# A wide form for two output units of each mixer, with the weights of the next unit but one prepared ahead of its eviction

## What is computed

```python
for i in range(DEPTH):                    # 4 layers: nsa, moba, conv, nsa
    x = x + mixer_i(rms_norm(x))          # ends in  o @ w_out,  1024 x 1024
    h = rms_norm(x)
    x = x + (silu(h @ w_gate) * (h @ w_up)) @ w_down
```

## Time and profile before

| | us |
|---|---|
| median of 3 runs | 2200.45 (2199.61 to 2200.75) |
| time of the profiled execution | 2200.64 |
| its span, first to last instruction | 2198.8 |
| PE busy | 2172.7 |
| DVE busy | 1783.2 |
| ACT busy | 1170.8 |

### The profile page before, as it was taken

One profiled execution on the slowest core, in us unless ns is written; L12 is line 12 of the kernel. 1 busy time (PEld: TensorE's weight loads), 2 busy tenths in 40 slices (PEclk: granted clock), 3 DMA queues, 4 the chain that ended last, 5 costly groups with the idle time before them and its releaser, 6 DMA issues.

```text
span 2198.8 us, 38037 instructions
## 1 busy us (share of the span) xinstructions
PE 2172.7 (99%) x15141; PEld 1946.7 (89%) x15141; DVE 1783.2 (81%) x3522; ACT 1170.8 (53%) x2051; POOL 0.2 (0%) x4
## 2 busy tenths in 40 slices
PE   9999999999999999999999999999999999999998
PEld 8888889898899988996988887898888889979998
DVE  8879978689887898888898777578877876478898
ACT  5776556565554655558655646453222236376533
POOL 0000000000000000000000000000000000000000
PEclk9999999999999999999999999999999999999999
DMA  8326665466665666670676531015454523435663
GB/s 272 123 84 235 222 213 193 166 210 234 196 220 176 208 237 201 220 222 22 229 236 201 178 125 58 20 61 181 157 187 167 166 80 106 135 98 166 208 236 120
DMA packets 115377, 372.04 MB, mean 169 GB/s; under 512 B 12416, under 2 KB 22272, under 8 KB 115200
## 3 DMA queue, kind: packets, MB, share of 16 engines
q1 hardware_dynamic: 106688, 359.97, 49.4%
q10 hardware_dynamic: 8512, 9.63, 1.4%
HBM read 367.46 MB, written 1.05 MB: 168 GB/s over the span
## 4 chain that ended last, share of the span: by engine, by line
PE 91%; DVE 6%; ACT 2%; issue 1%; DMA 0%; ACTq 0%; DVEq 0%; SPq 0%
PE ps L538 88%; DVE hid_f L2564 1%; PE ps L882 1%; DVE hid_f L2586 1%; PE ps L818 1%; PE ps L866 1%; DVE w_lo L2169 1%; PE ps L988 0%; ACT p_ring L1620 0%; DVE X L2301 0%; PE ps L806 0%; DVE a_both L2169 0%; DVE X L2448 0%; DVE recip L2580 0%; ACT hid_f L1687 0%
## 5 line engine op out<-in xcount | busy, mean ns | idle before, releaser
L538 PE MATMUL ps<-a_both,w_hi 128*128 128x256 f32 (+1 forms) x4816 | 1028.3, 328 | 1.4 <-DVE a_both L2169 0.7
L538 PEld LDWEIGHTS ps<-a_both,w_hi 128*128 128x128 f32 x4816 | 806.0, 190 | 78.0 <-DVE a_both L2169 3.4
L2169 DVE TENSOR_TENSOR w_lo<-w_raw,w_hi 128x1024 fp32r<-128x1024 f32 (+3 forms) x630 | 704.3, 1145 | 74.3 <-ACT w_hi L1480 58.3
L538 PE MATMUL ps<-a_both,w_lo 128*128 128x256 f32 (+1 forms) x3112 | 693.5, 292 | 0.0
L1480 ACT CAST w_hi<-w_raw 128x1024 fp32r<-128x1024 f32 (+3 forms) x428 | 403.8, 973 | 270.8 <-DMA w_raw<-weights 269.3
L538 PEld LDWEIGHTS ps<-a_both,w_lo 128*128 128x128 f32 x3112 | 506.3, 191 | 17.3
L538 PE MATMUL ps<-hid_both,w_hi 128*128 128x512 f32 (+2 forms) x2184 | 513.0, 347 | 0.7 <-DVE hid_both L2361 0.2
L538 PEld LDWEIGHTS ps<-hid_both,w_hi 128*128 128x128 f32 x2184 | 377.5, 189 | 54.4 <-issue 5.4
L538 PE MATMUL ps<-hid_both,w_lo 128*128 128x256 f32 (+2 forms) x1444 | 329.9, 304 | 0.0
L538 PEld LDWEIGHTS ps<-hid_both,w_lo 128*128 128x128 f32 x1444 | 229.8, 191 | 14.2
L1488 ACT CAST w_hi<-w_raw 128x1024 fp32r<-128x1024 f32 (+1 forms) x198 | 202.4, 1022 | 0.3 <-DMA w_raw<-weights 0.3
(11 more groups left out here) (261 smaller groups left out, 1938.9 us busy)
## 6 DMA issues: line engine op xcount, KB each, us to landing
w_raw<-weights SPq DMA_DIRECT2D x496, 512.0 KB, 4.5
pe_sb<-weights SPq DMA_DIRECT2D x96, 512.0 KB, 5.4
w_raw<-weights SPq DMA_DIRECT2D x64, 384.0 KB, 3.3
w_raw<-weights SPq DMA_DIRECT2D x64, 320.0 KB, 3.7
pe_sb<-na_bias ACTq DMA_DIRECT2D x32, 128.0 KB, 2.2
X<-x_t SPq DMA_DIRECT2D x2, 512.0 KB, 6.9
X<-c_rows ACTq DMA_DIRECT2D x2, 512.0 KB, 7.6
qk<-qk ACTq DMA_DIRECT2D x4, 256.0 KB, 6.2
```

The source lines that it names most:

```text
L538: return nc.tensor.matmul(out, stationary, moving, start=start, stop=stop)
L2169: return v.tensor_tensor(out, a, b.bitcast(F32), ALU.subtract)
```

## The change

Units o1 and o2 of all four mixers take the wide form. Unit o2 goes to ring A, o1 and o3 stay in D. PE issues all 16 high products of the unit, then the 16 low ones (`wide_unit`). On ACT and DVE, `mixer_ends` for these two units calls `ahead(u)` first; then ACT copies the low halves of both tiles in one instruction of 512 columns into `low_slot`, and DVE adds that copy to both tiles of `X` (512 columns, SBUF only), waits for itself, and adds the high halves from PSUM (512 columns). The tile work behind it is the same. Units o0 and o3 stay as they were, with `ahead(u)` behind.

```diff
+MIXER_WIDE = (1, 2)
...
+        def bank_pair(made):
+            lower = min(bank for bank, _, _ in made)
+            return slice(lower, lower + 2)
...
+            def wide_unit(ring, xs):
+                u, made = start_unit(2 * ring)
+                for _, p, _ in made:
+                    start_product(ring, p)
+                lower = bank_pair(made).start
+                for bank, _, _ in made:
+                    wide_highs(ps[:, bank, :], u % SLOTS, (bank - lower) * KD, xs, True, False)
+                for bank, _, (ready, _) in made:
+                    wide_lows(ps[:, bank, :], u % SLOTS, (bank - lower) * KD, xs, True).then_inc(ready, 1)
...
+                    if both and i in MIXER_WIDE:
+                        wide_unit("DA"[i - 1], both)
+                        continue
...
             def mixer_ends(gain, first="D"):            # ACT
+                before = None
                 for i in range(4):
-                    ring = first if i == 0 else "D"
+                    ring = first if i == 0 else "DAD"[i - 1]
                     u, made = next_unit(2 * ring)
                     if i == 3:
                         ready_sqrt()
+                    if i in MIXER_WIDE:
+                        ahead(u)
+                        for _, _, (s_, count) in made:
+                            wait(act, s_, count)
+                        if before:
+                            act.wait_ge(taken[before[0]], before[1] + 1)
+                        before = ring, made[1][1]
+                        nc.scalar.copy(low_slot, ps[:, bank_pair(made), S:2 * S]).then_inc(low_copied, 1)
                     for m in range(2):
                         residual_tile(made[m], 2 * i + m, gain, ring)
-                    ahead(u)
+                    if i not in MIXER_WIDE:
+                        ahead(u)
...
             def mixer_ends(gain, first="D"):            # DVE
+                    if i in MIXER_WIDE:
+                        ahead(u)
+                        for m in made:
+                            ready(m)
+                        n["low_part"] += 1
+                        dve.wait_ge(low_copied, n["low_part"])
+                        x = X[:, 2 * i:2 * i + 2, LAT]
+                        step(v.tensor_tensor(x, x, low_slot, ALU.add))
+                        sync()
+                        v.tensor_tensor(x, ps[:, bank_pair(made), 0:S], x, ALU.add).then_inc(taken[ring], 2)
+                    for m in range(2) if i not in MIXER_WIDE else ():
...
-                    ahead(u)
+                    if i not in MIXER_WIDE:
+                        ahead(u)
```

More of the change, by code:

```diff
@@ L699, in pairs, with out_units @@
                     fm_unit(rings, xs)
-            def out_units(src, tile_ready, between=None, begun=0, many=4, first="D"):
+            def wide_unit(ring, xs):
[7 more added lines that the diff above has]
+                    wide_lows(ps[:, bank, :], u % SLOTS, (bank - lower) * KD, xs, True).then_inc(ready, 1)
+            def out_units(src, tile_ready, between=None, begun=0, many=4, first="D", both=None):
                 for i in range(begun, many):
+                    if both and i in MIXER_WIDE:
+                        wide_unit("DA"[i - 1], both)
+                        continue
                     fm_unit(2 * ("D" if i else first), src, None if i else lambda k: pe.wait_ge(tile_ready, k + 1), i == 0,
@@ L1109, in run_nsa @@
                 pair_attention(f"nsa{j}", a, beside, 2, behind)
-                out_units(a, None, begun=1)
+                out_units(a, None, begun=1, both=wide_parts(LAT))
             def run_moba(_):
@@ L1206, in run_moba @@
                 out((4, 5, 6, 7))
-                out_units(src, None, begun=1)
+                out_units(src, None, begun=1, both=wide_parts(LAT))
             def run_conv(_):
@@ L1215, in run_conv @@
                     fm_unit("DD", a)
-                out_units([(by_hi[:, k, :], by_lo[:, k, :]) for k in range(KD)], conv_ready, first="A")
+                by = [(by_hi[:, k, :], by_lo[:, k, :], hid_both[:, :, S * k:S * k + S]) for k in range(KD)]
+                out_units([x[:2] for x in by], conv_ready, first="A", both=by)
             def gate_up(j, xs):
@@ L2539, in mixer_ends @@
                 for i in range(4):
-                    ring = first if i == 0 else "D"
+                    ring = first if i == 0 else "DAD"[i - 1]
                     u, made = next_unit(2 * ring)
-                    for m in range(2):
+                    if i in MIXER_WIDE:
[9 more added lines that the diff above has]
+                    for m in range(2) if i not in MIXER_WIDE else ():
                         bank = ready(made[m])
```

## The result

The change takes 2204.72 us (median of 10 runs, 2203.29 to 2207.22), the kernel before in the same session 2200.23 (10 runs, 2199.57 to 2200.92). The ratio is 1.0021 [1.0013, 1.0029] (95% interval): slower by 4.5 us, where 2.9 was forecast. The interval leaves out no change, though the difference is only 0.2%. The profiled execution took 2206.42, with a span of 2204.6, 5.8 longer than before.

The account below looks back on a forecast made before the run. PE was taken to bound the kernel, with DVE having hardly any reserve behind o3. Delays of 3 x 0.85 + 0.39 = 2.9 us, PE's saving already counted, on the median 2200.45 gave 2203.4; range 2199.0 to 2207.3.

Parts of the forecast that it names:

- PE's saving: In o1 and o2 a wide unit takes 5.57 us, 0.20 less than a narrow one; 1.6 us for eight units.
- The mechanism: DVE, behind splits and emptyings of o1 and o2, is late for the sums after o3; PE waits about 1.0 us.
- the hidden case: Emptying and splits keep ahead of PE in the mixers, only the saving shows: 2198.9 us; chance 0.10.
- all is hidden: Rival: emptying and splits keep ahead of PE in the mixers; total 2198.9 us, chance 0.10.
- The emptying: Behind o1 and o2 it holds DVE 1.42 us: SBUF addition 0.69, wait on itself 0.04, addition from PSUM 0.69.
- The landing: Casts of a unit's two weight halves start 3.86 and 5.09 us after the load starts; o3 has 0.1 to spare.
- the smaller delay: In conv, whose square root loads no table, the spread comes 0.39 us later, against 0.85 in the other mixers.
- slower, through landing: Rival: o3's second weight half lands late, each further 0.1 us costing 0.1 per mixer; 2207.4 at 1 us; chance 0.26.
- the prediction's own sign: If casts of o3 and f0 wait for DMA by more than 0.4 us, the landing case is right.
- The table load: Between o2's and o3's tiles, the small square root with its load holds ACT 1.49 us; conv 0.20 without load.
- The total: Spread later by 0.85 us in three mixers and 0.39 in conv: 2.9 in all, giving 2203.4 us.
- the landing case: Late landing of o3's weights delays every mixer's chain; 2207.4 us at 1 us later; chance 0.26.

Follow-up runs that it names:

- Order alone: The new order and rings with narrow units o1 and o2, against the kernel before: 2200.1 us, ratio 0.9998.
- one wide unit: Only o1 wide and prepared ahead, o2 narrow again with `ahead(u)` behind its tiles, against the kernel before: 2199.73 us, ratio 0.9998.
- the split in halves: The change with the second half of each `ahead(u)` put behind the emptying on both engines, against the kernel before: 2200.17 us, ratio 0.9996.
- the short loads: The change with only 64 columns loaded per half of o3's and f0's weights, against the kernel before: 2204.17 us, ratio 1.0018.
- the run with the late load: The change with o3's load held until the first `add_square` of o0, against the kernel before: 2213.65 us, ratio 1.006.
- both profiles of the change: The change's profiled execution, 2206.42 us, and a second one of the same change run again unaltered, 2207.35 us.

## Why the forecast was right, and where its sizes were off

**PE's saving** was right: 5.57 us for a wide unit, 0.40 for each mixer.

**The mechanism** was right. In nsa0 DVE empties o1 147.16 - 144.72 = 2.4 us after PE's end of it (1.9 forecast) and o2 153.45 - 150.29 = 3.2 after (2.6); in moba it is 444.64 - 442.74 = 1.9 and 450.92 - 448.31 = 2.6, as forecast. The table load stands where it was forecast, and PE waits at the sums in four places. Order alone and one wide unit cost nothing and two wide units do: the reserve that the earlier trace rows showed, 0.2 us at the sums and DVE's wait of 0.82 for o3's last tile, is used up by the second emptying. DVE's idle time in the three units is not: it is still 16.90 - 14.08 = 2.8 us in nsa0, but now DVE waits for ACT in it and not for PE, which is what the prediction held against the hidden case. Of the rivals, "all is hidden" falls for this order, though not for every order: with the split in halves it is what happens.

**The emptying** was 1.42 in the forecast; it measures 0.68 + 0.10 + 0.69 = 1.47 (from 147.16 to 148.63). The SBUF addition, 0.68, is near the value taken; the wait on itself, for which the forecast took 0.04 and had no row, is 0.10. Two of them add 0.1 a mixer.

**The landing** is the term that was mis-sized. It was priced from one pair of loads in conv, 5.09 us to the second cast, at a cost of 0.06 in every mixer. In nsa0 the same step takes 144.93 - 139.35 = 5.58, and there DVE waits 0.48 + 0.10 = 0.58 in the split of o3. In conv the forecast let the smaller delay stand because the square root loads no table there, but o3 cost 0.17 of waiting and f0 0.36 (from the casts of o2 DVE begins to empty o1 after 5.79 us and o2 after 12.44, against 5.62 and 11.91 with the short loads); so conv was at 0.97 instead of 0.39. With no landing in the chain, forecast and measurement agree: 0.85 - 0.06 + 0.10 = 0.89 (0.88 and 0.89 measured in three mixers), and 0.39 - 0.06 + 0.10 = 0.43 (0.44 measured in conv). So the rival "slower, through landing" is half true: it has its mechanism, at 1.2 us for the whole (4.27 - 3.10) instead of 4. By the prediction's own sign, casts that wait for DMA by more than 0.4 us, it holds in nsa0 (0.76 and 0.17 for o3) and in conv (0.33 and 0.19 for o3, 0.44 for f0).

Why o3's weights land later in nsa0 than elsewhere stays open. It isn't the load itself: started later, in the run with the late load, it took 144.75 - 140.28 = 4.47. The traces show one thing that goes with it. During this load there is one packet on q8, a queue of instructions (0.02 MB), in both profiles of the change, and during f0's load in conv in the first one, which took 6.26. Among the loads of o3 and f0 in all these runs, where the second cast waited for its load, it started 4.7 to 5.2 us after the load without such a packet and 5.3 to 6.3 with one, but for one of 4.74; the 5.09 of the earlier trace rows has such a packet too. That the packet is the cause is not shown.

**The table load** measures 157.91 - 156.50 = 1.41 from its start to the next activation with work, against the 1.49 counted; but it starts 156.50 - 154.96 = 1.54 after the first `a_hi` of the tiles ahead of it, against the 1.43 counted, so the two together are as forecast (2.95 and 2.92). The Trainium skill ("ScalarE: Activation LUTs", section "What ACT_TABLE_LOAD costs") would put a drain of about 1.38 on top of a load of 1.283; the traces have the load (1.28) and no room for the drain behind it, and the measurement decides.

**The total.** The forecast of 2.9 less the landing priced in it (4 x 0.06) and with the longer emptying (4 x 0.10) is 3.1; the landing measured adds 1.2, which gives the 4.27 of the chain. The range of the forecast was wide, from the hidden case to the landing case, and its chances put 0.68 on a difference within 4.4 us; the 4.5 measured lie on that bound and say nothing for or against the mechanism.

**What stays open**: the 0.2 us between the chain (4.27) and the medians (4.5); stretches in which nothing was changed differ by as much and more between two profiles (0.49 above). The lower clock after some waits fits the change's wider scatter (2203.29 to 2207.22, against 2199.57 to 2200.92 before), but only two of its executions were profiled; this is argued and not shown.

## What to carry to other kernels

Before an engine's preparation work is moved ahead of the emptying of a faster unit, follow the slower engine to the next point at which the bounding engine waits for all of its results: a saving of 0.2 us a unit was lost there because each emptying took 0.6 us more of DVE and arrived behind a whole split. Work split in two around the critical instruction cost nothing here, because its second half went into a wait that was there anyway. And the landing of a load is read for that load in that place, not taken from another: once its consumer stands ahead of the critical work, half a microsecond of landing is half a microsecond of the total.

## What the runs showed of the hardware

A wait of PE can be followed by a loss beyond its own length. With the late load, after waits of 2.00, 2.42 and 2.25 us the granted clock fell to the lower level (1.2 GHz) until about the spread, worth 1.05 to 1.37 us more; after 1.79 it did not; in the change, in the same place, it did not after 1.54 in one profile and did after 1.52 in the other, worth 1.0 more. After the waits of 0.95 to 1.01 us in the change's first profile it stayed at 1.00.
